# Two fused transformer blocks on one core: mLSTM mixer outputs by token tile, gate biases by accumulating DMA, second modulation as four rows, gate rows spread by one fp32r product

## What is computed

```python
sh1, sc1, g1, sh2, sc2, g2 = jnp.split(silu(c) @ ada_w + ada_b, 6, axis=-1)
hx = modulate(rmsnorm(x, pre_mix_g), sh1, sc1)
hc = modulate(rmsnorm(ctx, pre_mix_g), csh1, csc1)
yx, _ = mlstm_mixer(hx, hc, m_in_w, m_in_b, m_norm_g, m_out_w, False)
x = x + g1 * rmsnorm(yx, post_mix_g)
hx = modulate(rmsnorm(x, pre_ffn_g), sh2, sc2)
yx = conv_ffn(hx, ffn_up_w, ffn_conv_w, ffn_conv_b, ffn_down_w, True)
x = x + g2 * rmsnorm(yx, post_ffn_g)
```

```python
num = w_inter[..., None] * einsum('bhtd,bhde->bhte', qc, C) + einsum('bhts,bhse->bhte', s, vc)
den = w_inter * einsum('bhtd,bhd->bht', qc, n) + sum(s, axis=-1)
h = num / maximum(abs(den), exp(-m_t))[..., None]
```

## Time and profile before

| | |
|---|---|
| time, median of 3 runs | 860.15 us (859.45 to 860.78) |
| the profiled execution's own time | 859.28 us |
| its span | 857.6 us |
| PE busy | 815.4 us, 95% |
| DVE busy | 506.4 us, 59% |
| ACT busy | 384.0 us, 45% |
| POOL busy | 96.4 us, 11% |
| mean granted clock of TensorE | 0.984 of full speed |
| HBM read and written | 141.05 and 1.05 MB, 166 GB/s over the span |

### The profile page before, as it was taken

How to read it: one execution, slowest core, us unless ns; L and a number is a source line. 1 busy time by engine, 2 the same in 40 slices (tenths; PEclk the granted TensorE clock), 3 DMA queues, 4 the chain that set the end, 5 groups by cost and what they waited for, 6 DMA issues and landing times. The chain is left out here.

```text
span 857.6 us, 12818 instructions
## 1 busy us (share of the span) xinstructions
PE 815.4 (95%) x5214; PEld 724.6 (84%) x5214; DVE 506.4 (59%) x667; ACT 383.9 (45%) x520; POOL 96.4 (11%) x166
## 2 busy tenths in 40 slices
PE   3899999999899999999979999999989999999996
PEld 1678877887699999987869988988889999988885
DVE  0446789755486666686368785454555545554355
ACT  1542322433465655533356655446453443343373
POOL 3210211300100000000061313220100000000000
PEclk9999999989989999999999999999999999999999
DMA  9757476811346555568526242311445565555521
GB/s 328 282 207 259 150 252 229 290 50 50 98 131 191 172 193 196 187 231 298 168 58 192 99 148 69 109 71 50 144 163 174 194 195 170 175 170 192 176 99 49
DMA packets 102334, 142.74 MB, mean 166 GB/s; under 512 B 6167, under 2 KB 61968, under 8 KB 102288
## 3 DMA queue, kind: packets, MB, share of 16 engines
q1 hardware_dynamic: 96128, 136.33, 47.6%
q10 hardware_dynamic: 6160, 5.78, 2.0%
HBM read 141.05 MB, written 1.05 MB: 166 GB/s over the span
## 5 line engine op out<-in xcount | busy, mean ns | idle before, releaser
L1705 PE MATMUL ps<-h_hi,w_hi 128*128 128x256 f32 x864 | 247.4, 286 | 1.2 <-DVE h_lo L1141 0.6
L1706 PE MATMUL ps<-h_lo,w_hi 128*128 128x256 f32 x864 | 245.8, 284 | 0.0
L1707 PE MATMUL ps<-h_hi,w_lo 128*128 128x256 f32 x864 | 245.6, 284 | 0.0
L1120 DVE TENSOR_TENSOR w_lo<-raw,w_hi 128x2048 fp32r<-128x2048 f32 (+1 forms) x63 | 140.2, 2232 | 77.2 <-ACT w_hi L610 76.9
L1705 PEld LDWEIGHTS ps<-h_hi,w_hi 128*128 128x128 f32 x864 | 167.0, 193 | 2.5 <-issue 1.8
L1706 PEld LDWEIGHTS ps<-h_lo,w_hi 128*128 128x128 f32 x864 | 167.2, 194 | 0.0
L1707 PEld LDWEIGHTS ps<-h_hi,w_lo 128*128 128x128 f32 x864 | 167.1, 193 | 0.0
L610 ACT CAST w_hi<-raw 128x2048 fp32r<-128x2048 f32 (+1 forms) x63 | 116.8, 1854 | 101.2 <-PE ps L1707 59.4
L1128 DVE TENSOR_TENSOR w_lo<-raw,w_hi 128x2048 fp32r<-128x2048 f32 x44 | 100.7, 2289 | 61.1 <-ACT w_hi L618 61.1
L618 ACT CAST w_hi<-raw 128x2048 fp32r<-128x2048 f32 x44 | 83.6, 1899 | 50.5 <-PE ps L1707 50.5
L1705 PE MATMUL ps<-w_hi,h_hi 128*128 128x512 f32 x224 | 90.1, 402 | 0.7 <-DVE vb L1548 0.5
(11 more groups left out here) (349 smaller groups left out, 1088.2 us busy)
## 6 DMA issues: line engine op xcount, KB each, us to landing
raw<-in_ada_w SPq DMA_DIRECT2D x24, 1024.0 KB, 5.5
raw<-in_ffn_up_w SPq DMA_DIRECT2D x22, 1024.0 KB, 5.1
raw<-in_w_gate_up SPq DMA_DIRECT2D x22, 1024.0 KB, 5.1
raw<-in_w_in SPq DMA_DIRECT2D x14, 1024.0 KB, 5.2
raw<-in_m_in_w SPq DMA_DIRECT2D x12, 1024.0 KB, 5.2
raw<-in_ffn_down_w SPq DMA_DIRECT2D x10, 1024.0 KB, 5.1
raw<-in_w_down SPq DMA_DIRECT2D x10, 1024.0 KB, 5.1
raw<-in_m_out_w SPq DMA_DIRECT2D x4, 1024.0 KB, 5.4
```

Source lines behind the costliest of these rows:

```text
L1120: dve.tensor_tensor(part_view(w_lo, s), raw_view(split[s]), part_view(w_hi, s).bitcast(F32), ALU.subtract).then_inc(lo_ready, 1)
L1705: pe.matmul(dst, l_hi, r_hi, start=first, stop=False)
L1706: pe.matmul(dst, l_hi, r_lo, start=False, stop=False)
L1707: return pe.matmul(dst, l_lo, r_hi, start=False, stop=last)
```

## The change

1. `scores`: one fp32r product per direction spreads both rows at once (512 columns), in place of two fp32 products. For this ACT casts the rows to fp32r in partitions 0 to 3 of a new buffer `mw` and DVE writes the remainder into partitions 32 to 35; `sel` has 64 rows and is made of a constant by a copy on DVE at the start.
2. `outputs` runs token tile by token tile, with banks 4 and 5 for tile 0 and 6 and 7 for tile 1, and signals each tile; `head_out` works tile by tile; a tile of `outputs(h)` waits only for the same tile of head h - 1. On DVE `head_out(2)` now stands before `gated_head(1)`.
3. `gate_vector` has no products for the bias. POOL adds `ada_b` to partition 0 of the gathered sums by an accumulating DMA (`add_gate_bias`), behind its `weighted_keys(3)` for g1 and behind its work for `post1` for g2.
4. sh2 and sc2: four products with 32 columns of ones give four rows in bank 2, side by side in partitions 0, 32, 64 and 96. ACT copies them out and starts four small transfers that fold them to 16 rows of 128; PE transposes these between the two halves of the product with m_out_w, and DVE adds bias and gain there.
5. `tmp` is gone (the last stage uses the memory of `sil`), and three semaphores become one (`p_step`).

```diff
             def scores(h):
                 if h == 0:
-                    pe.wait_ge(S("w_row"), 2)
+                    pe.wait_ge(S("w_row"), 4)
...
-                    pe.matmul(ps[:, 5 + d, 0:T], sel[:, h, :], m_row[:, d, :], start=True, stop=True)
-                    pe.matmul(ps[:, 5 + d, T:2 * T], sel[:, h, :], w_row[:, d, :], start=True, stop=True)\
-                        .then_inc(S("m_bcast"), 1)
+                    pe.matmul(ps[:, 5 + d, :], sel[:, h, :], mw[:, :, d, :], start=True, stop=True).then_inc(S("m_bcast"), 1)
```

```diff
 # ACT, behind w_row
+            act.wait_ge(S("w_row"), 2)
+            act.copy(mw[0:MH].rearrange("p v d t -> p (v d t)"), junk[0:MH, :]).then_inc(S("w_row"), 1)
 # DVE, behind lo_until(6)
+            dve.wait_ge(S("w_row"), 3)
+            dve.tensor_tensor(mw[32:32 + MH].rearrange("p v d t -> p (v d t)"), junk[0:MH, :],
+                              mw[0:MH].rearrange("p v d t -> p (v d t)").bitcast(F32), ALU.subtract).then_inc(S("w_row"), 1)
 # POOL, constants
+            link(pool.memset(mw[:].bitcast(F32), 0.0))
+            link(pool.memset(sel_f, 0.0))
+            link(keep(sel_f, ALU.not_equal, [[-1, MH], [0, P]], 1, fill=1.0))
+            keep(sel_f, ALU.not_equal, [[-1, MH], [0, P]], 1, fill=1.0, base=-32).then_inc(S("const_ready"), 1)
 # DVE, behind first_diagonals(0)
+            dve.wait_ge(S("const_ready"), 2)
+            link(dve.tensor_copy(sel[:], sel_f))
```

```diff
             def outputs(h):
                 pe.wait_ge(S("prob_ready"), 2 * h + 2)
                 pe.wait_ge(S("state_out"), 2 * MH)
-                if h:
-                    pe.wait_ge(S("h_sum"), 2 * h)
-                for d in range(2):
-                    pr = prob[:, h, d, :]
-                    for t in range(TT):
-                        dst = ps[:, 4 + 2 * d + t, 0:DV + 1]
+                for t in range(TT):
+                    if h:
+                        pe.wait_ge(S("h_sum"), 2 * h - 1 + t)
+                    for d in range(2):
+                        pr = prob[:, h, d, :]
+                        dst = ps[:, 4 + 2 * t + d, 0:DV + 1]
...
-                ins.then_inc(S("out_mm"), 1)
+                    ins.then_inc(S("out_mm"), 1)
             def gate_vector(v, bank):
+                pe.wait_ge(S("ada_bias"), 16 if v == 0 else 32)
                 for n in range(2):
-                    pe.matmul(ps[:, bank + n, :], ones[:], ada_acc[v][:, n * NB:(n + 1) * NB], start=True, stop=False)
-                    for j in range(4):
-                        c = col["ada_b"] + (2 + v) * KD + 4 * n + j
-                        ins = pe.matmul(ps[:, bank + n, j * P:(j + 1) * P], cols[:, c:c + 1].to_broadcast([P, P]), ident[:],
-                                        start=False, stop=j == 3)
+                    ins = pe.matmul(ps[:, bank + n, :], ones[:], ada_acc[v][:, n * NB:(n + 1) * NB], start=True, stop=True)
 # POOL
+            def add_gate_bias(v):
+                pool.wait_ge(ada2_used, 4 * v + 4)
+                pool.dma_start(ada_acc[v][0:1, :], I["ada_b"][0:1, (2 + v) * D:(3 + v) * D], accum_op=ALU.add)
```

```diff
 # PE, behind outputs(1)
-            for j in range(2 * KD):
-                ins = pe.matmul(ps[:, 2, j:j + 1], ada_acc[1 + j // KD][:, (j % KD) * P:(j % KD + 1) * P], ones[:, 0:1],
+            pe.wait_ge(ada2_used, 12)
+            for j in range(4):
+                ins = pe.matmul(ps[32 * j:32 * j + 32, 2, :], ones[:, 0:32], ada_acc[1 + j // 2][:, j % 2 * NB:(j % 2 + 1) * NB],
                                 start=True, stop=True)
...
             outputs(2)
-            pe.wait_ge(S("mods_out"), 2)
+            pe.wait_ge(S("mods_out"), 3)
...
             pe.wait_ge(S("h_sum"), 2 * MH)
+            pe.wait_ge(S("small_in"), 16 * 6)
+            flip(ps[:, 7, 0:2 * KD], mod_rows).then_inc(S("ada_sum"), 1)
 # ACT, behind head_squares(1)
+                    act.wait_ge(S("ada_sum"), 2)
+                    act.copy(mod_sums, ps[:, 2, :]).then_inc(S("mods_out"), 1)
+                    act.wait_ge(S("mods_out"), 3)
+                    for j in range(4):
+                        load(mod_rows[4 * j:4 * j + 4, :], mod_sums[32 * j:32 * j + 1, :].rearrange("o (k p) -> o k p", p=P), "small_in")
 # DVE
             head_out(1)
-            <bias and gain of sh2, sc2>
             gated_head(0)
+            head_out(2)
             gated_head(1)
-            head_out(2)
```

More of the change, by code:

```diff
@@ L457, in _ @@
             link(pool.memset(row_of[:], 0.0))
-            for m in (s_le_t, s_ge_t, s_lt_t, s_gt_t, ones, sel):
+            for m in (s_le_t, s_ge_t, s_lt_t, s_gt_t, ones):
                 link(pool.memset(m[:], 1.0))
@@ L469, in _ @@
             link(keep(s_gt_t[:], ALU.is_gt, [[-1, P]], 1))
-            keep(sel[:], ALU.is_equal, [[-1, MH], [0, P]], 1).then_inc(S("const_ready"), 1)
+            link(pool.memset(mw[:].bitcast(F32), 0.0))
+            link(pool.memset(sel_f, 0.0))
+            link(keep(sel_f, ALU.not_equal, [[-1, MH], [0, P]], 1, fill=1.0))
+            keep(sel_f, ALU.not_equal, [[-1, MH], [0, P]], 1, fill=1.0, base=-32).then_inc(S("const_ready"), 1)
             for i in range(2):
@@ L496, in causal @@
                     keep(pr[:, 2 * P:], ALU.is_ge, [[sign, P]], -sign).then_inc(S("prob_ready"), 1)
+            def add_gate_bias(v):
+                pool.wait_ge(ada2_used, 4 * v + 4)
+                pool.dma_start(ada_acc[v][0:1, :], I["ada_b"][0:1, (2 + v) * D:(3 + v) * D], accum_op=ALU.add)                    .then_inc(S("ada_bias"), 16)
             def weighted_keys(h):
@@ L517, in _ @@
             weighted_keys(3)
+            add_gate_bias(0)
             for h in range(MH):
@@ L530, in _ @@
             post_norm("post1", "norm2")
+            add_gate_bias(3)
             post_norm("post2", "norm3")
@@ L1073, in _ @@
                         act.wait_ge(S("x_upd"), 16 + i - 1)
-                    bank_out(tmp[:, i % 2, :], i, "sig_ready", ACT.Sigmoid)
+                    bank_out(sig[:, i % 2, :], i, "sig_ready", ACT.Sigmoid)
                     if n == 1:
@@ L1345, in head_out @@
                     dve.wait_ge(S("emt_ready"), 1)
-                dve.wait_ge(S("out_mm"), h + 1)
-                num_den = ps[:, 4:8, DV].rearrange("p (d t) -> p d t", d=2)
-                by_d = den[:, 0, :].rearrange("p (d t) -> p d t", d=2)
-                floor = emt[:].rearrange("p (t d) h -> p d t h", d=2)[:, :, :, h]
-                link(dve.scalar_tensor_tensor(by_d, num_den, -1.0, floor, ALU.mult, ALU.max))
-                link(dve.tensor_tensor(by_d, by_d, num_den, ALU.max))
-                link(dve.reciprocal(den[:, 1, :], den[:, 0, :]))
-                for t in range(TT):
+                for t in range(TT):
+                    dve.wait_ge(S("out_mm"), TT * h + t + 1)
+                    num_den = ps[:, 4 + 2 * t:6 + 2 * t, DV]
+                    two = slice(2 * t, 2 * t + 2)
+                    link(dve.scalar_tensor_tensor(den[:, 0, two], num_den, -1.0, emt[:, two, h], ALU.mult, ALU.max))
+                    link(dve.tensor_tensor(den[:, 0, two], den[:, 0, two], num_den, ALU.max))
+                    link(dve.reciprocal(den[:, 1, two], den[:, 0, two]))
                     hs = hsum[:, t, h * DV:(h + 1) * DV]
-                    link(dve.tensor_scalar(hs, ps[:, 4 + t, 0:DV], den[:, 1, t:t + 1], None, ALU.mult))
-                    dve.scalar_tensor_tensor(hs, ps[:, 6 + t, 0:DV], den[:, 1, TT + t:TT + t + 1], hs, ALU.mult, ALU.add)\
+                    link(dve.tensor_scalar(hs, ps[:, 4 + 2 * t, 0:DV], den[:, 1, 2 * t:2 * t + 1], None, ALU.mult))
+                    dve.scalar_tensor_tensor(hs, ps[:, 5 + 2 * t, 0:DV], den[:, 1, 2 * t + 1:2 * t + 2], hs, ALU.mult, ALU.add)\
                         .then_inc(S("h_sum"), 1)
@@ L1397, in _ @@
             transposed("y1", (0, 1, 0, 1), lambda k: pcol("m_norm", k), pairs=range(2, MH))
+            lo_until(at["mix_out"][1] + 2)
+            dve.wait_ge(S("ada_sum"), 3)
+            bias2 = cols[:, col["ada_b"] + 3 * KD:col["ada_b"] + 5 * KD]
+            link(dve.tensor_tensor(mod2[:], ps[:, 7, 0:2 * KD], bias2, ALU.add))
+            link(dve.scalar_tensor_tensor(mod2[:, KD:], mod2[:, KD:], 1.0, cols[:, col["pre_ffn"]:col["pre_ffn"] + KD],
+                                          ALU.add, ALU.mult))
             lo_until(at["mix_out"][1] + 3)
@@ L1433, in _ @@
             lo_until(at["down"][1] + 2)
[L1434 removed]
+            dve.wait_ge(S("ada_sum"), 4)
             times_gate(0, gp2)
@@ L1670, in _ @@
             s_next[0] = V0 + 2 * PAIRS + 3
-            dve.wait_ge(S("p_T"), 1)
-            dve.tensor_copy(pT[:].rearrange("p k t -> p (k t)"), ps[:, 6, :]).then_inc(S("pT_ready"), 1)
-            dve.wait_ge(S("p_hi"), 1)
-            lo_part(p_lo[:], pT[:], p_hi[:], "p_lo")
+            dve.wait_ge(S("p_step"), 1)
+            dve.tensor_copy(pT[:].rearrange("p k t -> p (k t)"), ps[:, 6, :]).then_inc(S("p_step"), 1)
+            dve.wait_ge(S("p_step"), 3)
```

(7 more changed lines are left out.)

24 lines of the change are left out of this document (10 added, 14 removed).

## The result

The changed kernel takes 856.89 us (median of 8 runs, 854.73 to 860.39) against 860.5 us for the kernel before (8 runs): ratio 0.9944, 95% interval 0.9927 to 0.996. The ratio is not the quotient of the two medians: it stands for 4.8 us less, the medians differ by 3.6. A second set gave 855.43 against 859.95 us and again 0.9944 (0.9925 to 0.9964). The forecast was 848.3 us, with a range of 845.5 to 853.0: the sign was right, the size was not. The profiled execution took 857.36 us, with a span of 855.6 and a mean clock of 0.983; before it was 859.28, 857.6 and 0.984.

The account below looks back on a forecast made before the run. PE, busy 95% of the span, was taken to set the time, with DVE nearly as full in the mixer. 5.84 - 2.35 + 1.78 + 3.46 + 2.38 - 0.85 - 0.2 + 1.78 = 11.8 us off 860.15 gave 848.3, range 845.5 to 853.0.

Parts of the forecast that it names:

- Spreading: Gate rows in `scores`: fp32r pair at 0.57 us saves 1.46 us per head, 5.84 for four, less a 2.35 us wait.
- Behind it, the o block, the states and `outputs(0)` find their inputs ready; 3.45 us stay.: After the new wait at the o block's start, PE waits for nothing more up to `outputs(0)`; 3.45 us remain saved.
- a rival at 0.23: New waits of 2.35 and 2.2 us bring the clock down: one fall 850 to 851.8, both up to 855; chance 0.23.
- Gate biases: `gate_vector(0)` and `gate_vector(3)` without bias products: 1.78 us less each, the second if its transfer is in time.
- I take 3 us and no wait: The accumulating transfer ahead of `gate_vector(3)` lands in 3 us, with 5.1 us available, so PE does not wait.
- The rival on the slower side: Accumulating transfer bounds `gate_vector(3)`, slower from 18.6 us to landing upward; at 20 us, 863 us in all; chance 0.03.
- Second modulation: Four rows at 1.06 us replace 16 column products, 3.46 us less; `outputs(2)` at full clock, 2.38 us less.
- Outputs by tile: From `outputs(2)`'s end to the m_out_w product: 8.6 us against 7.7, costing 0.85, with waits before `y_pair(1)` and `y_pair(2)`.
- DVE isn't the wall: Rival: DVE runs ahead at the o block, or `y_pair(1)` isn't late; 845 to 846 us; more won, chance 0.07.
- Flip: PE's transpose of the second modulation's 16 rows, within the m_out_w product, costs about 0.2 us.
- What is won in the mixer should reach the end.: Work from 240 us on is almost all PE's, so the mixer's gain should reach the end; no size of its own.
- the change does little of what it says: Rival: fp32r product costs as much as the old four, and the clock falls in the waits; 856.9 us; chance 0.04.

Follow-up runs that it names:

- b_scores: The kernel before with the fp32r spread of the gate rows alone: 861.28 us, ratio 1.0007.
- b_outputs: The kernel before with outputs by token tile and `head_out(2)` ahead of `gated_head(1)` alone: 861.26 us, ratio 1.001.
- a_vmid: The changed kernel with `v_evac(1)` between the second modulation's partial sums and the subtraction of `lo_until(10)` on DVE: 852.36 us, ratio 0.9891.
- a_lo15: The changed kernel with DVE's subtraction of slice 14 behind the last transposed pairs instead of ahead of `gated_head(2)`: 854.11 us, ratio 0.993.
- a_vfirst: The changed kernel with `v_evac(1)` ahead of the weight subtraction of `lo_until(10)` on DVE: 856.87 us, ratio 0.9958.
- a_gate2: The changed kernel with `gate_vector(3)` behind the first slice of the second half of down, not before it: 853.22 us, ratio 0.9918.
- b_rows: The kernel before with the second modulation's four side-by-side rows alone: 859.44 us, ratio 0.9972.

## Why the prediction was wrong in size

- **Spreading.** Per head 1.27 us, not 1.46: scores to next block 2.88 us before and 115.71 - 114.10 = 1.61 now. The pair costs 0.66 in place of 0.57, and the block's first product still takes 0.34 us, not 0.23. With the wait for `v_evac(1)` (1.62 and 2.17 us in the two profiles) the o block starts 2.02 and 1.47 us earlier against `scores(0)`. The forecast was 4.38 - 2.35 = 2.03; the first profile meets it because the saving and the wait were both smaller.
- **"Behind it, the o block, the states and `outputs(0)` find their inputs ready; 3.45 us stay."** (5.84 - 2.35 is 3.49, as the sum has it.) This is the step that failed first, and the largest: 0.4 us stayed in one profile and -0.2 in the other. The clock fell in the o block: 7.18 us between its start and `scores(3)`, where it was 5.58 before. I had this as a rival at 0.23 and a price of at least 1.7; it is 1.6. And POOL, whose rows I read only for free time, was slowed by DVE's subtractions and kept PE waiting 1.05 and 1.12 us. b_scores has neither the fall nor that wait, and there 3.47 us stayed.
- **Gate biases.** 1.72 us at the first, and at the second 36.22 us from `gate_vector(3)` to norm 3 before and 34.51 now: 1.71. Both as forecast. "I take 3 us and no wait" failed: the transfer of 4 KB took 5.7 us from issue to landing in the first profile, and the 20 of the ten profiles took 4.0 to 6.1; where PE waited, it cost 0.7 to 1.3 us. The size of a transfer isn't its price; the nearest row was of another queue. The rival on the slower side stayed far off. The 620 and 3100 ns that I took from the Trainium skill ("SBUF — State Buffer") stand there in the section "A bandwidth-pool intuition that's wrong (but worth ruling out)"; whether such a lock-out is part of the 5.7 us no run here shows.
- **Second modulation.** Four rows took 1.0 us and `outputs(2)` 4.44: both terms (3.46 and 2.38) held in their place. But the 2.38 was not a saving that reached the end: the mean clock was 0.984 before and 0.983 and 0.985 after. What the clock gave in one place it took in the o block and near 512 us. Nor is the fall tied to the columns, as b_outputs and a_vmid show, so how much of this term is due to taking them out stays open.
- **Outputs by tile.** Forecast +0.85 us, measured 202.11 - 192.56 = 9.55 against 7.74, so +1.8. The wait before `y_pair(1)` was right, that before `y_pair(2)` was 0.9 too short, because POOL was held: in a_lo15, where it isn't, `y_pair(2)` doesn't wait. "DVE isn't the wall" is refuted by the two waits themselves, and by a_vfirst.
- **Flip.** 0.2 us forecast; norm 2's first tile comes 0.08 us later against `y_pair(3)`, and its second 0.33 us later against the first.
- **"What is won in the mixer should reach the end."** This failed as well. From norm 3 to norm 5 the changed kernel is 1.8 to 1.9 us slower with the same work, and has the clock at 0.57 from 512 to 516 us, where a_gate2 has 1.00. A forecast can't be held to where such falls come, but its range can, and mine had no term for falls outside the edited places.

Sum over the edited stretches: 11.8 forecast, 7.0 and 6.1 found. Of the 4.9 us missing in the first profile, 3.1 are missing up to `outputs(0)`, 1.1 up to `y_pair(3)` and 0.8 up to norm 3. The spans are 2.0 and 3.5 us shorter, the rest being lost in stretches without an edit: to the falls near 77 and 512 us in the first profile, and to the one near 512 us and 0.8 us ahead of `scores(0)` in the second. For the 4.8 us of the runs this is inferred, since they have no profile each.

The measured 856.89 us is next to the 856.9 of the rival "the change does little of what it says". That is chance: the half of its condition that is worth most, an fp32r spread as dear as the old four products, is refuted by the 0.66 us; of the falls in the waits one came.

**Open.** Why the clock fell behind the wait at the o block in all five profiles of the changed order that kept it and not in b_scores, which waits 1.49 us at the same place, wasn't settled; none of the profiles without that wait has a fall between 140 and 146 us. The length of a wait doesn't decide it: the clock stayed up behind the wait of 2.54 us in a_vfirst, and behind 3.28 us at the second norm in b_rows (16 transposes in 2.05 us), where the prediction had 2.94 us as a length that brings it down. Whether the start of norm 3 itself decides on the fall near 512 us, or something that moves with it, wasn't tried by a pause of its own. The profiles differ by up to 4.2 us ahead of `scores(0)`. Most of it is a fall at 74 us: from the first product with `wg_parts` (54.75 to 56.40 us) to `scores(0)` PE takes 56.2 us in the seven profiles without it and 57.6 to 59.2 in the seven with it, for the same work. As near 512 us, it goes with the time of arrival: the six profiles that come to `wg_parts` first, at 55.47 us or earlier, have no fall, the six that come last, at 55.77 or later, have it, and of the two in between, 0.01 us apart, one has it. With one profile per kernel how often each has it isn't known, so the table's first column says nothing about an edit.

## What to carry to other kernels

Where two engines are both nearly full, price an edit by the whole chain of the second one: what its next three consumers wait for, and who runs beside it, not only the first wait. Then clear the waits that the edit makes and those beside them: four small moves of the order tripled the gain, by the ratios from 4.8 to 15.0 us. And compare profiles by stretches between fixed instructions, since a median hides that a gain was real and was lost elsewhere: the spread gave 3.5 us in its stretch alone and nothing in the time.

## What was not expected of the hardware

- A 128 x 2 multiplication on GpSimd took 2.13 us in place of 0.19 when it was issued 0.2 us after VectorE's 128 x 2048 subtraction, and eight multiplications of 128 x 128 took 6.42, 8.12 and 9.83 us with no, one and two whole subtractions beside them.
- An accumulating transfer of 4 KB from GpSimd's queue landed 4.0 to 6.1 us after its issue, later than 256 KB from ACT's queue (3.0 us).
- The granted clock's falls are not bound to one cause in the program: the same 16 narrow products stood behind a fall to 0.72 over 12 us in one kernel and behind 1.00 in another, and the same stages near 74 and 512 us ran at half or at full clock, in step with the time at which PE came to them. Behind the wait of 2.0 us before `y_pair(1)` it fell in one profile and stayed up in six.
